# Prompt attention in chunks of 512 keys with a running maximum, with two more tiles in flight

## What is computed

```
s = jnp.einsum('ntkgch,nskch->nkgcts', q, k) * SCALE          # c = 0, 1: two score maps per head
s = jnp.where(k_pos[None, :] <= q_pos[:, None], s, -jnp.inf)
p = jax.nn.softmax(s, axis=-1)
a = p[:, :, :, 0] - lam * p[:, :, :, 1]
o = jnp.einsum('nkgts,nskv->ntkgv', a, v)
```

## Time and profile before

| what | value |
|---|---|
| median of 3 runs | 2523.19 us (2513.9 to 2526.07) |
| the profiled execution's own time | 2513.99 us |
| its span | 2512.2 us |
| busy in the span: PE, DVE, ACT, POOL | 2172.5, 1174.0, 973.7, 1315.0 us |
| prompt attention, all 16 heads | about 1512 to 2108 us of the span |
| mean granted TensorE clock of the span | 0.910 of 2.4 GHz |

### The profile page before, as it was taken

One profiled execution on the slowest core, in us unless ns is written; L12 is line 12 of the kernel. 1 busy time (PEld: TensorE's weight loads), 2 busy tenths in 40 slices (PEclk: granted clock), 3 DMA queues, 4 the chain that ended last, 5 costly groups with the idle time before them and its releaser, 6 DMA issues. The chain is left out here.

```text
span 2512.2 us, 37652 instructions
## 1 busy us (share of the span) xinstructions
PE 2172.5 (86%) x13193; PEld 1994.9 (79%) x13193; DVE 1174.0 (47%) x1908; ACT 973.7 (39%) x1573; POOL 1315.0 (52%) x687
## 2 busy tenths in 40 slices
PE   4999999999356998999989997778777777897998
PEld 4999999999346998999889995656666666666998
DVE  3698889888876003222100005555555564336001
ACT  4455555555443112111112115555555554223111
POOL 2799999999765324334311225555465562124232
PEclk7999999999568998999999997888788888998999
DMA  6121111212222222222223331001000004882221
GB/s 232 50 60 58 59 59 59 67 42 67 68 69 77 84 59 104 77 93 68 92 88 94 101 111 43 18 17 34 17 25 17 9 1 132 253 259 88 60 82 72
DMA packets 182030, 192.43 MB, mean 77 GB/s; under 512 B 11434, under 2 KB 147059, under 8 KB 181331
## 3 DMA queue, kind: packets, MB, share of 16 engines
q1 hardware_dynamic: 181952, 191.48, 24.2%
HBM read 145.52 MB, written 47.63 MB: 77 GB/s over the span
## 5 line engine op out<-in xcount | busy, mean ns | idle before, releaser
L222 POOL TENSOR_TENSOR w_lo<-w_raw,w_hi 128x1024 fp32r<-128x1024 f32 x120 | 289.9, 2417 | 647.1 <-ACT w_hi L218 647.1
L233 PE MATMUL ps<-Hhi,w_hi 128*128 128x352 f32 x1704 | 560.0, 329 | 18.8 <-POOL w_lo L222 12.2
L233 PE MATMUL ps<-Hhi,w_lo 128*128 128x352 f32 x1704 | 549.8, 323 | 0.0
L233 PE MATMUL ps<-Hlo,w_hi 128*128 128x352 f32 x1704 | 548.9, 322 | 0.0
L218 ACT ACTIVATE w_hi<-w_raw 128x1024 fp32r<-128x1024 f32 x120 | 126.2, 1053 | 717.4 <-PE ps L833 278.5
L768 DVE SCALAR_TENSOR_TENSOR ps<-U,dww,ps 128x512 f32<-128x512 f32 x608 | 403.0, 744 | 0.0
L687 POOL TENSOR_TENSOR pool_acc<-pool_acc,prod 128x1024 f32<-128x1024 f32 x144 | 346.3, 2405 | 31.0 <-ACT prod L636 22.7
L233 PEld LDWEIGHTS ps<-Hhi,w_hi 128*128 128x128 f32 x1704 | 321.4, 189 | 28.7 <-POOL w_lo L222 19.0
L233 PEld LDWEIGHTS ps<-Hlo,w_hi 128*128 128x128 f32 x1704 | 322.3, 189 | 2.4 <-issue 0.5
L233 PEld LDWEIGHTS ps<-Hhi,w_lo 128*128 128x128 f32 x1704 | 321.3, 189 | 0.0
L636 ACT ACTIVATE prod<-U,dww 128x1024 f32<-128x1024 f32 x176 | 197.0, 1147 | 250.1 <-POOL pool_acc L687 143.5
(11 more groups left out here) (227 smaller groups left out, 3727.6 us busy)
## 6 DMA issues: line engine op xcount, KB each, us to landing
w_raw<-conv_w_in SPq DMA_DIRECT2D x48, 512.0 KB, 3.9
w_raw<-attn_w_in SPq DMA_DIRECT2D x40, 512.0 KB, 4.5
kpage<-cache_k SPq DMA_DIRECT2D x64, 256.0 KB, 2.9
vpage<-cache_v SPq DMA_DIRECT2D x64, 256.0 KB
res<-Y SPq DMA_DIRECT2D x2, 4224.0 KB, 20.5
gate<-sg SPq DMA_DIRECT2D x16, 528.0 KB, 4.0
sgl<-gate SPq DMA_DIRECT2D x16, 528.0 KB, 3.6
xres<-res SPq DMA_DIRECT2D x16, 528.0 KB, 3.7
```

What stands on the lines that cost most here:

```text
L222: pool.tensor_tensor(wlo[s][:, :, :], raw[s][:, :, :], whi[s][:, :, :].bitcast(F32), ALU.subtract).then_inc(w_lo, 1)
L233: mm = pe.matmul(ps[:, 3 * dst + c, 0:CH], w[:, k, :], r(k)[:, c * CH:(c + 1) * CH], start=start and k == 0 and w is whi[s] and r is rhs_h ...
```

## The change

It does the following.

- A wide tile is cut into two units, the first 512 keys and the rest (`parts`, `unit_of`, `width`). Each unit takes one pair of banks; units alternate between the two pairs, so scores wait only for the exponentials of the unit before last.
- The maximum of the second unit is joined with that of the first (`min` of negated maxima, then `sub`, L1658 and L1661), and the second unit's exponentials use it. ACT then makes the weight exp(old maximum - new maximum) for both maps at once (`weight`, L1583).
- `coefficients` forms the sums and factors of a wide tile in five instructions that depend on each other (L1670 to L1678); a narrow tile keeps two. The squares of the sums are taken once per head (L1681). The function now stands between the maxima of the first and the second unit.
- POOL scales the first 512 columns of both maps (L1730, L1732) and the rest of `p1` (L1734), then joins (L1737).
- LAG is 3; `p1` has four buffers, two of them in other places; `stats` has a place of its own for every tile of a group. VALUES, OUTPUTS, TOTALS, SUMS and NEW_VALUES move by one or two steps.
- The nine semaphores of the prompt's first loads become five (`X_GROUPS`): tiles 2 and 3, 4 and 5, 6 to 8 are awaited together.

```diff
-        stats = place("stats", [P, 4, 8], F32, at)
-        p1 = [place(f"p1_{s}", [P, NP_TOK], F32, [raw_at[s]]) for s in range(2)]
+        stats = place("stats", [P, GH * QT, 20], F32, at)
+        p1 = [place("p1_0", [P, 5 * P], F32, p1_at), place("p1_1", [P, NP_TOK], F32, slot(44)),
+              place("p1_2", [P, NP_TOK], F32, [raw_at[0]]), place("p1_3", [P, NP_TOK], F32, [raw_at[1]])]
...
-        LAG = 2
-        VALUES = {8: (0, (0,)), 9: (0, (1, 2, 3)), 10: (1, (0, 1)), 11: (1, (2, 3)), 12: (1, (4, 5)), 13: (1, (6, 7))}
-        OUTPUTS, TOTALS, SUMS = {9: 0, 13: 1}, {10: 0, 14: 1}, {11: 0, 15: 1}
-        NEW_VALUES = 6
+        LAG = 3
+        VALUES = {9: (0, (0,)), 10: (0, (1, 2, 3)), 11: (1, (0, 1)), 12: (1, (2, 3)), 13: (1, (4, 5)), 14: (1, (6, 7))}
+        OUTPUTS, TOTALS, SUMS = {11: 0, 15: 1}, {12: 0, 16: 1}, {13: 0, 17: 1}
+        NEW_VALUES = 7
...
+        def score_ap(x, n, c):
+            return ps[:, 2 * (unit_of(x, n) % 2) + c, 0:width(x, n)]
...
+                    if u >= 2:
+                        pe.wait_ge(exp_done, 2 * NU * g + 2 * (u - 2) + 2)
...
                     if x < top and not late:
-                        scores(g, x)
+                        scores(g, x, 0)
                     if 0 <= x - LAG < top:
-                        turn(g, x - LAG)
+                        turn(g, x - LAG, slice(0, 1))
+                    if x < top and parts(x) == 2:
+                        scores(g, x, 1)
+                    if 0 <= x - LAG < top:
+                        turn(g, x - LAG, slice(1, 2))
...
                     if x < top:
-                        exp(g, x, 0)
-                        exp(g, x, 1)
+                        for c in range(2):
+                            exp(g, x, 0, c)
+                    if 0 <= x - LAG < top:
+                        hi(g, x - LAG, slice(0, 1))
+                    if x < top and parts(x) == 2:
+                        for c in range(2):
+                            exp(g, x, 1, c)
+                        weight(g, x)
...
+                    if n == 1:
+                        dve.wait_ge(mx_done, 2 * NU * g + 2 * u + 2)
+                        dve.tensor_tensor(stat(x, N_NM + 2, 2), stat(x, N_NM, 2), stat(x, N_NM + 2, 2), ALU.min
+                                          ).then_inc(run_done, 1)
+                        dve.wait_ge(run_done, 4 * GH * g + wides(x) + 1)
+                        dve.tensor_tensor(stat(x, N_D, 2), stat(x, N_NM + 2, 2), stat(x, N_NM, 2), ALU.subtract
+                                          ).then_inc(dist_done, 1)
...
+                    if wide:
+                        dve.wait_ge(weight_done, 4 * GH * g + wides(x) + 1)
+                        step_up(dve.tensor_tensor(stat(x, N_ES, 2), stat(x, N_E, 2), stat(x, N_SA, 2), ALU.mult))
+                        step_done()
+                        step_up(dve.tensor_tensor(stat(x, N_S, 2), stat(x, N_ES, 2), stat(x, N_SB, 2), ALU.add))
+                        step_done()
+                    dve.tensor_tensor(stat(x, N_T0), stat(x, N_S), neglam, ALU.mult).then_inc(rc_done, 1)
+                    dve.reciprocal(stat(x, N_R1), stat(x, N_S + 1)).then_inc(rc_done, 1)
+                    if wide:
+                        dve.wait_ge(rc_done, 20 * GH * g + coefs(x) + 1)
+                        dve.tensor_tensor(stat(x, N_U), stat(x, N_T0), stat(x, N_E + 1), ALU.mult).then_inc(rc_done, 1)
...
+                    if x < top:
+                        maxes(g, x, 0)
                     if 0 <= x - 1 < top:
-                        coefficient(g, x - 1)
-                    if x < top:
-                        maxes(g, x)
+                        coefficients(g, x - 1)
+                    if x < top and parts(x) == 2:
+                        maxes(g, x, 1)
                     if 0 <= x - LAG < top:
                         lo(g, x - LAG)
...
+                    if last:
+                        pool.tensor_scalar(b[:, 0:512], b[:, 0:512], stat(x, N_U), stat(x, N_R1),
+                                           ALU.mult, ALU.mult).then_inc(pn_done, 1)
+                        pool.tensor_scalar(a[:, 0:512], a[:, 0:512], stat(x, N_E), 1.0,
+                                           ALU.mult, ALU.mult).then_inc(pn_done, 1)
+                    pool.tensor_scalar(b[:, last:w], b[:, last:w], stat(x, N_T0), stat(x, N_R1),
+                                       ALU.mult, ALU.mult).then_inc(pn_done, 1)
+                    pool.wait_ge(pn_done, 16 * GH * g + x + 1 + 2 * wides(x + 1))
+                    pool.tensor_tensor(a[:, 0:w], a[:, 0:w], b[:, 0:w], ALU.add).then_inc(comb_done, 1)
```

More of the change, by code:

```diff
@@ L1404, in tgroups, with parts, unit_of, wides @@
             return [(first + n, 4 * n, min(4, i + 1 - 4 * n)) for n in range(i // 4 + 1)]
[L1406 to L1410, removed]
+        def parts(x):
+            return 1 if x % QT < 4 else 2
+        def unit_of(x, n):
+            return tgroups(x)[n][0]
+        def wides(x):
+            return 4 * (x // QT) + max(0, x % QT - 4)
+        def width(x, n):
+            return min(512, P * (x % QT + 1) - 512 * n)
+        def score_ap(x, n, c):
+            return ps[:, 2 * (unit_of(x, n) % 2) + c, 0:width(x, n)]
+        def stat(x, c0, n=1):
+            return stats[:, x % NX, c0:c0 + n]
+        def coefs(x):
+            return 2 * x + wides(x)
         with nc.Block() as block:
@@ L1443, in scores @@
                         pe.wait_ge(qlo_ready, GH * g + j + 1)
[L1445 to L1452, removed]
-                    dst = [score_ap(i, c) for c in range(2)]
-                    for n, (ql, kr) in enumerate(((qhi, khi), (qhi, klo), (qlo, khi))):
-                        for c0 in range(0, w, 512):
-                            c1 = min(w, c0 + 512)
-                            for c in range(2):
-                                rows_ = slice(HD * c, HD * c + HD)
-                                pe.matmul(dst[c][:, c0:c1], ql[s][rows_, i * P:(i + 1) * P], kr[rows_, c0:c1],
-                                          start=n == 0, stop=n == 2 and c1 < w)
@@ L1461, in scores @@
-                    for c in range(2):
-                        pe.matmul(dst[c][:, i * P:w], identr[:, :], causalr[:, :], start=False, stop=True
-                                  ).then_inc(s_done, 1)
-                def turn(g, x):
+                    if u >= 2:
+                        pe.wait_ge(exp_done, 2 * NU * g + 2 * (u - 2) + 2)
+                    dst = [score_ap(x, n, c) for c in range(2)]
+                    masked = n == parts(x) - 1
+                    for m, (ql, kr) in enumerate(((qhi, khi), (qhi, klo), (qlo, khi))):
+                        for c in range(2):
+                            rows_ = slice(HD * c, HD * c + HD)
+                            mm = pe.matmul(dst[c], ql[s][rows_, i * P:(i + 1) * P], kr[rows_, 512 * n:512 * n + w],
+                                           start=m == 0, stop=m == 2 and not masked)
+                            if m == 2 and not masked:
+                                mm.then_inc(s_done, 1)
@@ L1466, in turn @@
+                    if masked:
+                        for c in range(2):
+                            pe.matmul(dst[c][:, w - P:w], identr[:, :], causalr[:, :], start=False, stop=True
+                                      ).then_inc(s_done, 1)
+                def turn(g, x, which):
                     pe.wait_ge(comb_done, NX * g + x + 1)
-                    for tg, b0, nb in tgroups(x):
+                    for tg, b0, nb in tgroups(x)[which]:
                         if tg >= 2:
```

98 lines of the change are left out of this document (59 added, 39 removed).

## The result

| | before | after |
|---|---|---|
| median of 8 runs each, us | 2516.57 (2512.67 to 2526.07) | 2532.07 (2528.09 to 2535.72) |
| the profiled execution's own time, span, us | 2513.99, 2512.2 | 2533.21, 2531.4 |

The changed kernel takes 1.005 times as long (95% interval 1.003 to 1.0071): 15.5 us slower by the medians, 19.2 by the profiled executions. The forecast was 16 us faster than the profiled execution before; by that the sum missed by 35 us.

A forecast was written before the change was run, and what follows sets the result against it. The prediction took a chain of waits, no engine full, to bound the kernel. 8 x 34.4 + 3 x 36.0 + 3 x 37.65 + 33 gave 529 us against 545.0, so 2507 us (range 2465 to 2545).

The forecast's parts named there:

- Exclusion and lockstep: Wide tiles: two-input DVE and POOL instructions exclude each other, so both alternate; join 4 to join 7 takes 22.3 us.
- J: Stretch of a head from the start of join 4 to the end of join 7, forecast at 22.3 us.
- Two kinds of head differ ... 1.6 more: 36.0: A group's first head: v_hi on ACT makes the second narrow maximum late, 1.6 us over the ordinary 34.4.
- Then PE carries the head: 0.12 to start: After join 7: PE starts tile 7's turn 0.12 us later, at full clock, 12.1 us until join 4 starts again.
- R: Stretch from the end of join 7 to the next start of join 4, forecast at 12.1 us in ordinary heads.
- The clock rival: PE's clock stays low into tile 7's turn and first values, some 1.6 us in 11 heads: 2538 us, chance 0.17.
- The caught factor: Rival at the first narrow tile: T0 waits for join 7's whole sum, 1.6 us a head: 2520 us, chance 0.25.
- The ring: Scores, maxima and exponentials waiting in turn, 3.77 us; the change opens it, PE's 77.2 us wait for ACT nearly gone.
- The products: POOL's wide-tile joins: the added products add 1.1 us each, 4.5 a head.
- Key blocks: Heads where the key block changes: k_hi, k_lo and first scores in sequence, 3.25 us more, 37.65 for 42.1 before.
- The drain: End of the stage: the deeper LAG gives one step more to drain, under 1 us.
- A deeper LAG: Counted among the edits at no cost, apart from one more step to drain, under 1 us.

The follow-up runs named there:

- E2: Changed kernel with VectorE's minimum, difference, sums and factors of wide tiles, and T0, given one tensor input: 2494.77 us, ratio 0.9904 to the kernel before.
- E3: Changed kernel with the next head's queries' split moved from the step of tile 4 to that of tile 2: 2498.37 us, ratio 0.992.
- E1: Changed kernel with the subtraction for the new values' low part moved from GpSimd to VectorE: 2513.47 us, ratio 0.9975 to the kernel before.
- E5: Changed kernel with extra TensorE transposes of the identity, 24 in the step of tile 7 and 12 in the next tile 0: 2523.6 us, ratio 1.0022.
- C2: C1 with extra transposes, 8 in the step of tile 7 and 20 in that of tile 0: 2455.92 us, ratio 0.9757.
- E4: Changed kernel without the two added products by the weight, so wide tiles get a wrong weight: 2512.63 us, ratio 0.9971.
- E6: Changed kernel with LAG back at 2 and the steps that move with it as before the change: 2631.25 us, ratio 1.0442.
- E8: Changed kernel with the loop over the groups written out on four engines: 2522.24 us, ratio 1.0022 to the kernel before.
- E7: Changed kernel with the edits of E1 and E5 together: 2510.17 us, ratio 0.9966 to the kernel before.
- C3: C2 with the loop over the groups written out: 2444.45 us, ratio 0.9718 to the kernel before.
- C1: Changed kernel with the edits of E1, E2 and E3 together: 2469.19 us, ratio 0.9798 to the kernel before.

## Why the prediction was wrong

- **Exclusion and lockstep: right.** J was forecast at 22.3 us and took 20.8 in all but a few heads. Its hand-overs (0.62 and 0.81 us) are those of the text; the 1.5 too much is 0.2 per join for DVE's instructions let in between, which delayed nothing visible, and 0.1 to 0.2 in each join's own length. S waits some 2 us behind the split in 13 of 15 heads, as forecast; POOL's busy share is 0.66, not three quarters. E2 and E3 show that the exclusion and the queries' split were on the path, as the text had it.
- **"Two kinds of head differ ... 1.6 more: 36.0": this step failed most.** The text charged a group's first head for `v_hi` on ACT. `v_lo` on POOL, which the same move puts behind join 7 (2.35 us) and in front of the first narrow join and of PE's values, it did not charge. Such heads took 41.1 us, 5.1 more than forecast, four times (three stand in the sum as such, the fourth as the filling head). E1 takes 19 us out by moving that one instruction.
- **"Then PE carries the head: 0.12 to start": the second failure.** In the kernel before, the turn of tile 7 begins 0.13 to 0.17 us behind join 7 in all eight ordinary heads. In the changed one PE is not there when join 7 ends: the turn begins 1.4 to 2.4 us late, 1.9 in the mean. In the head of the windows above PE stands still for half of 1731 to 1734, and the clock is at 0.50. It stays there to 1740 with PE at work nearly without a break, so the transposes of tile 7 begin 1.5 us late (against 1740.37):

```profile
1732.98 1.11 PE L1494 MATMUL ps<-small,p 128*128 128x128 f32 x4 [1.53 <-DVE aTlo L1689]
1738.92 1.47 DVE L1674 TENSOR_TENSOR stats<-stats,misc 128x1 f32<-128x1 f32 x1
1741.88 1.07 PE L1494 MATMUL ps<-small,p 128*128 128x128 f32 x8
```

The text's argument against this, that the clock "was back some 2 us after such a start", did not hold: PE starts again at 1732.98, and the window from 1734 to 1738 still shows 0.50. The chain behind the transposes takes 12.9 us, not 12.0 (the terms of the text add to 12.18, not 12.1). R is 14.7 for 12.1, against 1.5 saved in J: 1.2 us more for each of eight heads, 10 us. E5 shows the clock's part: 2.1 us in the head where the level held, 1.4 where it fell late; in C2, where it holds in all eight, 2.0.

- **The clock rival** named the right cause and lay nearest the result (2538 for 2532), but that it lay so near is luck: its price was made of the wrong parts. It let the turn of tile 7 and the values behind it take twice as long; in the head above they run at the full clock, 1.07 us for the eight transposes, and what is slow is PE's work ahead of them. The caught factor, which it includes at 1.6 us a head, did occur (1.47 us at 1738.92) but costs little: PE goes into the turn of tile 7 without an idle gap in 15 of the 16 heads, and R of E2, where the factor is not caught, is only 0.3 shorter. The 20 us of the first heads it does not have.
- **The ring:** said to be "nearly gone", 45.0 of the 77.2 us stayed, most of it as one wait of 3.1 us ahead of the scores of tile 7, in 12 of the 16 heads. ACT's exponentials of tile 6 wait for DVE's min, which stands behind S, which stands behind POOL's queries' split. The first two lines show this in the changed kernel; the third is PE's line in E3, which moves the split:

```profile
1762.16 0.58 ACT L1578 ACTIVATE p<-ps,stats 128x384 f32<-128x384 f32 x1 [2.94 <-DVE stats L1658]
1763.45 0.50 PE L1479 MATMUL ps<-khi,qhi 64*128 64x512 f32 x2 [3.10 <-ACT p L1578]
...
PE ps L1479 <- ACT p L1578: 25.6, 52, 1.0
```

The ring was opened at the banks and closed again by the exclusion of DVE and POOL. It is not what makes PE late at join 7: R of E3's ordinary heads is 14.8.

- **The products "each add 1.1 us, 4.5 a head":** true of POOL's busy time. Without them an ordinary head is 1.0 us shorter (E4), with the new wait of 2.0 us in it.
- **Key blocks:** 37.65 forecast, 38.2 measured. **The drain:** "under 1 us" was 1.6. **"A deeper LAG" at no cost:** right, but it was no side edit: without it the change costs 113 us (E6).
- **Not in any rival:** the standstill at the loop's start, 2.75 us in two groups (E8).

Of the 35 us by which the sum missed, the first heads make 20 and the ordinary ones 10; key heads, filling, drain and the stages behind make the rest. E7, with `v_lo` moved and PE less late, is 9 us below the kernel before, where the sum had 16: the two failures, turned back, restore the sign of the forecast and half of its size, with 5.7 us of standing at the loop's start still in it.

## What to carry to other kernels

When an instruction moves in one engine's order, charge all that the same table entry moves on the other engines, and ask what is queued behind it there. Before letting an engine "carry" a stretch, look at its clock and its backlog in the microseconds before: an engine that arrives late makes a shorter wait worth nothing. In a kernel like this one, small factors on VectorE beside a busy GpSimd are better given one tensor input, with per-partition scalars for the others (E2).

## What was not expected of the hardware

- A one-input VectorE instruction on one column, with one or two scalars from SBUF, takes 0.20 to 0.27 us and never waited for GpSimd (E2, 576 cases); the two-input form takes 0.16 us alone and up to 2.3 behind GpSimd's split (the changed kernel).
- After the loop's jump back an engine can stand still with its operands ready: DVE for 2.75 us in the changed kernel, PE for up to 3.6 us in C2. Written out, these waits are gone (E8, C3). The jump alone does not make them: the kernel before, E3 and C1 jump back too, and their lists have no such wait of DVE or PE over 0.3 us. The Trainium skill, "Runtime: NRT & Kernel Launch", Instruction fetch mechanics, says that a taken branch to a target outside the current window of two pages makes the engine wait for a fetch. The runs agree that it takes the jump; that the fetch is the cause no run here shows.
- The granted clock can fall well after the standstill, while PE is at work: in E5 it is 1.00 from 1618.7 to 1620.2 and 0.50 from 1621.7, with PE busy throughout. Extra transposes moved that fall and kept it away in one head of E5; with less waiting around them they kept a mean of 0.95 (C2 and C3).
